# A stick-breaking attention's diagonal masks moved from Pool to VectorE, and a new order for the last expert

## The reference, cut to what matters

```python
z = einsum('bqhd,bkhd->bhqk', q, k) * SB_SCALE
visible = k_pos[None, :] < q_pos[:, None]              # strictly causal
log_skip = where(visible, log_sigmoid(-z), 0.0)
between = cumsum(log_skip, axis=3, reverse=True) - log_skip
weight = where(visible, exp(log_sigmoid(z) + between), 0.0)
out = einsum('bhqk,bkhd->bqhd', weight, v)
...
hh = silu(x @ w_gate[e]) * (x @ w_up[e]) * comb[e]      # per expert e
y = y + hh @ w_down[e]
```

## Time and profile before

| | |
|---|---|
| median of 3 runs | 870.22 us (869.53 to 870.33) |
| the profiled execution | 869.36 us |
| its span, first to last instruction | 867.6 us |
| PE busy | 820.0 us, 95% |
| DVE, ACT, POOL busy | 319.5, 233.7, 183.5 us |
| mean granted PE clock | 0.995 |
| DMA | 155.78 MB |

### The profile page before, as it was taken

The page is one execution under the profiler, slowest core; times in us unless marked ns, Lnnn a source line. Parts: engine busy times, 40 slices in busy tenths (PEclk is TensorE's granted clock), DMA queues, the critical chain, the costliest instruction groups (busy, mean ns, idle before and its releaser), DMA issues.

```text
span 867.6 us, 11942 instructions
## 1 busy us (share of the span) xinstructions
PE 820.0 (95%) x4635; PEld 504.8 (58%) x4635; DVE 319.5 (37%) x917; ACT 233.7 (27%) x483; POOL 183.5 (21%) x225
## 2 busy tenths in 40 slices
PE   6989999999899999899999999999799999999885
PEld 4465444688665765576676677455555555555452
DVE  5222555999643542122232336435621111111100
ACT  3021232112333333234333350212222222222211
POOL 3223440000332322200000001100124334343222
PEclk9999999999999999999999999999999999999998
DMA  8624020412200200210304059844789999999994
GB/s 285 170 98 129 3 99 0 151 57 94 98 1 0 98 1 0 78 28 1 146 1 97 1 189 412 321 159 149 280 308 393 397 400 398 397 395 398 401 405 146
DMA packets 59544, 155.78 MB, mean 180 GB/s; under 512 B 15384, under 2 KB 22008, under 8 KB 52320
## 3 DMA queue, kind: packets, MB, share of 16 engines
q1 hardware_dynamic: 50912, 141.74, 43.6%
q0 software_dynamic: 8576, 13.28, 5.7%
HBM read 147.10 MB, written 15.99 MB: 188 GB/s over the span
## 4 chain that ended last, share of the span: by engine, by line
PE 79%; DMA 5%; POOL 3%; DVE 3%; SPq 3%; ACT 3%; issue 2%; POOLq 0%; DVEq 0%; ACTq 0%
PE quad L866 18%; PE pair L1201 9%; PE quad L1336 6%; PE quad L1456 5%; PE pair L1456 5%; PE pair L1064 5%; PE quad L936 3%; DMA arena<-in_w_up 3%; PE pair L1469 3%; PE quad L1469 3%; PE pair L856 2%; PE quad L1158 2%; SPq L732 2%; POOL arena L1940 2%; PE pair L983 2%
## 5 line engine op out<-in xcount | busy, mean ns | idle before, releaser
L866 PE MATMUL quad<-ring_w,xnT 128*128 128x512 f32 (+1 forms) x192 | 79.3, 553 | 0.0
L1064 PE MATMUL pair<-xnT,ring_w 128*128 128x272 f32 x256 | 70.6, 411 | 0.9 <-POOLq L1946 0.9
L1201 PE MATMUL pair<-xnT,ring_w 128*128 128x272 f32 x256 | 65.8, 403 | 0.0
L2004 POOL DMA_INDIRECT out_y_prompt<-ring_w,idx x32 | 50.8, 1586 | 65.2 <-ACT ring_w L1817 63.3
L866 PE MATMUL quad<-xnT,ring_w 128*128 128x280 f32 (+1 forms) x256 | 60.6, 396 | 0.0
L1064 PEld LDWEIGHTS pair<-xnT,ring_w 128*128 128x128 f32 x256 | 46.7, 194 | 16.9 <-issue 7.9
L2247 DVE CUSTOM_DVE_ANT_0 arena<-quad,arena 128x528 f32<-128x528 f32 (+4 forms) x34 | 17.7, 520 | 103.9 <-PE quad L1256 60.9
L1201 PEld LDWEIGHTS pair<-xnT,ring_w 128*128 128x128 f32 x256 | 46.5, 189 | 15.3 <-issue 6.9
L866 PEld LDWEIGHTS quad<-xnT,ring_w 128*128 128x128 f32 x256 | 48.2, 190 | 10.8 <-issue 0.4
L1999 POOL DMA_INDIRECT ring_w<-xn_d,idx x32 | 33.2, 1038 | 95.8 <-PE quad L1447 45.9
L866 PEld LDWEIGHTS quad<-ring_w,xnT 128*128 128x128 f32 x192 | 34.3, 189 | 31.7 <-issue 26.1
(11 more groups left out here) (285 smaller groups left out, 1239.9 us busy)
## 6 DMA issues: line engine op xcount, KB each, us to landing
arena<-in_w_gate SPq DMA_DIRECT2D x21, 1024.0 KB
arena<-in_w_up SPq DMA_DIRECT2D x21, 1024.0 KB
arena<-in_w_down SPq DMA_DIRECT2D x40, 512.0 KB
ring_w<-in_w_in SPq DMA_DIRECT2D x8, 2048.0 KB, 8.5
ring_w<-in_w_down SPq DMA_DIRECT2D x20, 512.0 KB, 21.7
xnT<-in_w_gate SPq DMA_DIRECT2D x4, 1024.0 KB
xnT<-in_w_up SPq DMA_DIRECT2D x4, 1024.0 KB
ring_w<-in_w_in SPq DMA_DIRECT2D x3, 1024.0 KB, 7.3
```

The costliest lines, as they stand in the source:

```text
L866: last = nc.tensor.matmul(o, l, r, start=i == 0, stop=i == len(mms) - 1)
L1064: last = nc.tensor.matmul(bank[6 + job % 2][:, 0:hi - lo], chunk8(6 + cb // 4)[:, k, c0:c0 + P], xT[:, k, lo:hi], start=k == 0, stop=k == ...
L1201: last = nc.tensor.matmul(bank[6 + job % 2][:, 0:hi - lo], w[:, k, c0:c0 + P], rhs[:, k, lo:hi], start=k == 0, stop=k == kt - 1)
L2004: pool.indirect_dma_start(yp_half, bass.IndirectOffsetOnAxis(ap=rows, axis=0), Yb[:, q, :], None, bounds_check=2 * SEQ - 1, oob_is_err=Fal ...
```

## The change

Three things.

1. Pool masks nothing in the stage. DVE adds -1e30 (`BIG` times a 0/-1 triangle that is already in SBUF) to the masked scores in PSUM, ahead of the clamp, once per diagonal step: one instruction for a prompt step, two for the sample step and for the tail. The clamp, exp, ln and the maximum then give 0 for these elements, and so does the exponential for the weights. PE waits for `sp_ready` and `w_ready` in every step.
2. Before the gather's wait `keep_busy(6)` becomes `keep_busy(4)`.
3. For the last expert (n = 31) PE turns its hidden values between the two halves of the down product of expert 30, and does the sample's sum for expert 29 right after that product, ahead of the down product of 31.

```diff
@@ PE, stage @@
-                    if s["diag"]:
-                        pe.wait_ge(w_masked, s["diags"])
-                    else:
-                        pe.wait_ge(w_ready, m + 1)
+                    pe.wait_ge(w_ready, m + 1)
...
-                    if s["diag"]:
-                        pe.wait_ge(sp_masked, s["diags"])
-                    else:
-                        pe.wait_ge(sp_ready, m + 1)
+                    pe.wait_ge(sp_ready, m + 1)
...
-            keep_busy(6)
+            keep_busy(4)
@@ PE, experts @@
-            def down(q, slot, done):
+            def down(q, slot, done, between=None):
                 for f in range(2):
+                    if f and between is not None:
+                        between()
...
+                def turn_hidden():
+                    pe.wait_ge(hid_ready, n + 1)
+                    hidden_to_width(n % 2, hT_ready)
+                if n == NE - 1:
+                    down_in_turn(n - 1, turn_hidden)
+                    add_sample_in_turn(n - 2)
+                    break
                 if n:
                     down_in_turn(n - 1)
-                pe.wait_ge(hid_ready, n + 1)
-                hidden_to_width(n % 2, hT_ready)
+                turn_hidden()
             down_in_turn(NE - 1)
-            for n in range(NE - 3, NE):
+            for n in range(NE - 2, NE):
                 add_sample_in_turn(n)
@@ Pool, stage: mask() and its two calls are gone @@
-                    if s["diag"]:
-                        p0, p1 = s["p0"], s["p0"] + s["nk"]
-                        pool.wait_ge(sp_ready, i + 1)
-                        mask(spt[p0:p1] if s["kind"] == "tail" else spb[p0:p1, i % SPR], s)
-                        nc.gpsimd.sem_inc(sp_masked, 1)
...
-                    if s["diag"]:
-                        p0, p1 = s["p0"], s["p0"] + s["nk"]
-                        pool.wait_ge(w_ready, m + 1)
-                        mask(wtt[p0:p1] if s["kind"] == "tail" else wtb[p0:p1, m % WR], s)
-                        nc.gpsimd.sem_inc(w_masked, 1)
@@ DVE, stage @@
+            def not_before(z, s):
+                p0, p1 = s["p0"], s["p0"] + s["nk"]
+                if s["kind"] == "prompt":
+                    q0 = 0 if s["j"] else N_META
+                    w = P - q0
+                    return [(ntri[:, q0:P].rearrange("p (o q) -> p o q", o=1).broadcast_to([P, 2, w]), z[:, :, 0:w])]
+                nq = DEC if s["kind"] == "sample" else N_TAIL
+                later = ntri[p0:p1, p0:p0 + nq].rearrange("p (o q) -> p o q", o=1).broadcast_to([p1 - p0, NPAIR, nq])
+                return [(later, z[:, u, :].rearrange("p (b q) -> p b q", b=NPAIR)) for u in range(2)]
...
                 dve.wait_ge(z_ready, i + 1)
+                if s["diag"]:
+                    for later, z_diag in not_before(z, s):
+                        ins = nc.vector.scalar_tensor_tensor(z_diag, later, BIG, z_diag, ALU.mult, ALU.add)
+                    link(ins)
```

More of the change, by code:

```diff
@@ L151, in sb_steps @@
         s["closes"] = s["last"] and s["kind"] != "tail"
-        s["diags"] = sum(t["diag"] for t in steps[:i + 1])
     for i, s in enumerate(steps):
@@ L482, in build @@
         sp_ready = sem("sp_ready")
-        sp_masked = sem("sp_masked")
         suf_init = sem("suf_init")
@@ L1473, in down, with down_in_turn @@
                 last.then_inc(done, 1)
-            def down_in_turn(n):
+            def down_in_turn(n, between=None):
                 pe.wait_ge(hidT_ready, n + 1)
@@ L1479, in down_in_turn @@
                     pe.wait_ge(y_copied, n - 1)
-                down(n % 2, n % MS, y_done)
+                down(n % 2, n % MS, y_done, between)
             def add_sample(q, first, last, done):
@@ L1904, in _ @@
             pool.wait_ge(keys_out, 16 * 6 * (NT + 1))
[L1905 to L1918, removed]
-                    p0, p1 = s["p0"], s["p0"] + s["nk"]
-                    v = v.rearrange("p u (b q) -> p (u b) q", b=NPAIR)
-                    later = stri[p0:p1, p0:p1].rearrange("p (o q) -> p o q", o=1).broadcast_to([N_TAIL, 2 * NPAIR, N_TAIL])
-                    link(nc.gpsimd.tensor_tensor(v, v, later, ALU.mult))
-            for i in range(NSTEP + 1):
-                if i < NSTEP:
-                    s = STEPS[i]
-                    if s["diag"]:
-                        p0, p1 = s["p0"], s["p0"] + s["nk"]
-                        pool.wait_ge(sp_ready, i + 1)
-                        mask(spt[p0:p1] if s["kind"] == "tail" else spb[p0:p1, i % SPR], s)
-                        nc.gpsimd.sem_inc(sp_masked, 1)
+            for i in range(NSTEP + 1):
                 m = i - 1
```

## The result

| | before | after |
|---|---|---|
| median, runs of one chip | 869.88 us (869.45 to 870.33, 4 runs) | 860.13 us (859.22 to 861.20, 4 runs) |
| ratio | | 0.9885 [0.9868, 0.9903] |
| profiled execution, its span | 869.36 us, 867.6 us | 859.87 us, 858.0 us |
| PE, DVE, POOL busy | 820.0, 319.5, 183.5 us | 818.4, 327.0, 168.8 us |

The account below looks back on a forecast made before the run. TensorE and its waits bound the kernel up to the experts, the weight stream from there on. Stage 9.2 + last expert 0.55 - filler's clock fall 1.2 = 8.55 us less than 870.22: forecast 861.6 us, range 859.2 to 864.5.

Parts of the forecast that it names:

- The bound: Whole kernel: TensorE and its waits up to the experts, then the weight stream; time gained before the experts moves the end equally.
- The stalls, 8.4: Stick-breaking stage: TensorE's 13 waits for Pool vanish, 7.5 us of idle time plus 0.9 us of lost overlap.
- The clock in the stage, 1.66: Stick-breaking stage: the low clock after the longest stall (1.79 us, before 329.39) goes with that stall, gaining 1.66 us.
- The mask, 0.52 a step and 0.85 in all: VectorE's mask ahead of the clamp: 0.48 us plus 0.04 wait per step, costing 0.85 us where ScalarE's slack is short.
- the three places: Stage steps with little ScalarE idle time before its weights (226.28, 284.70, 326.40): would pay 0.52, 0.10 and 0.24 us.
- The filler, -1.2: Before the gather: two fewer filler calls lengthen TensorE's idle to 2.6 us, the clock likely falls, costing 1.2 us (0 to 1.7).
- rival 1: At the gather: the clock holds despite the longer idle gap, giving 860.4 us; chance 0.32.
- The last expert, 0.55: Kernel's end: ScalarE's copy of y(31) no longer waits for the sample's sum of expert 29, gaining 0.55 us (0 to 0.9).
- The sum: Whole kernel: 9.2 for the stage + 0.55 for the last expert - 1.2 for the filler = 8.55 us less.
- Rival 4: Stage: the added mask paces every step, slower than before from a mask of about 3.2 us, about 880 at 3.5; chance 0.02.

Follow-up runs that it names:

- the filled stall: Kernel before, with throwaway products filling the longest stall (1.8 us, step 17's product with the values), the wait itself kept: 869.66 us, ratio 0.9989.
- four masks: Changed kernel with VectorE's mask issued four times in each diagonal step, the masked values unchanged: 873.95 us, ratio 1.0042 against the kernel before.

## Why the prediction was right, step by step

**The bound.** Right. From the gate and up product of the second expert to the last scatter it took 225.1 us before (634.25 to 859.37) and 224.6 to 225.3 in the thirteen other profiles, although it began at times between 624.1 and 635.5. What is gained or lost before the experts arrives at the end.

**The stalls, 8.4.** Right, and confirmed from two sides: the wait for Pool vanished, and turning Pool's order alone brought 8.05, the clock's share included. Put side by side, instruction by instruction, the two profiles give 8.63 for the stalls: 7.65 us of idle time and 14 times the 0.07 of overlap. The one that I hadn't counted is at 346.07, with 0.12 us too short for a bracket.

**The clock in the stage, 1.66.** Measured 1.65 by the filled stall.

**The mask, 0.52 a step and 0.85 in all.** It took 0.43 + 0.03 = 0.46. The price in the stage is 0.64, the difference to the kernel that keeps it off ScalarE's chain. Two of the three places paid, 0.24 and 0.40 where I had about 0.5 and 0.24; at the third (282.15, before: 284.70) ScalarE's idle time went to nothing, and TensorE didn't wait. The stage adds up: 8.63 + 1.65 - 0.64 is 9.64, and 9.62 was measured where I had 9.2.

**The filler, -1.2: the step that failed.** I let the clock fall after 2.6 us of idle time and took 1.2 us off the gain. The gap was 2.46 us and the clock held, as in rival 1 (860.4, with a chance of 0.32; 860.13 was measured). So the forecast of 861.6 stood for the wrong one of the two cases, and is near because the case was worth little. The filler alone gave 1.0003, with 3.06 us of gap and no fall. The price was of the right size, if low (1.4 to 1.7 in the four profiles where a low clock reached the experts' start); the cause was not.

Idle times just before the gather and what followed, by profile: 1.65, 1.71, 2.00, 2.46 and 3.06 us passed, 1.70, 1.81 and 1.89 were followed by a fall. The length of the gap does not order these. (In five of the other six the clock had fallen in or just before the filler, which then took longer and left 0 to 0.9 us; from the gather to the second gate and up product these took the full-clock 6.54, so a fall there cost nothing. The sixth is the 4.99.)

Over the whole of the 14 profiles, after the first 20 us, 10 of the 28 idle times of TensorE of 1.75 to 3.1 us that began at full clock were followed by a fall, and 1 of the 46 of 1.5 to 1.75. So the length does count, and by this count a fall at 2.46 us was a chance of about a third and not likelier than not. In 11 of the 14 profiled executions the clock was low for a time between 604 and 632 us, in three of them twice, at different places for the same program, and 11 of the falls there had no idle time over 0.82 us just before them. Against that, the 1.8 us stall at 330 was followed by a fall in all three profiles that have it.

The Trainium skill ("TensorE: Matmul & The Clock Gate", section "What's actually happening") says that the point of a transition depends on when the work arrives against a monitor that runs freely; the two profiles of the changed kernel agree with that, since at 612.5 the same idle times were followed by a fall in one and not in the other. By the rule on gaps of the same page of the Trainium skill (section "Why this matters for your kernels"), weighed in the prediction, 2.46 us was safe: so it was in this trace, but 2.16 us at 808 in the same trace was not, nor were 1.70 to 1.89 us in the others.

**The last expert, 0.55.** The mechanism gave 0.54 from the start of the product of 30 on. What I left out is when that product starts. I had put the last expert after the arrival of the last weights, but the product of 30 waits for its own w_down, which lands last but one. In the change's first profile that made it start 0.24 us later after the gate and up product than before, so 0.30 net; in its second profile 0.03 later, and 0.51 net. Between the five profiles with the old last expert (10.06 to 10.38 us from gate and up to scatter) and the eight with the split (9.53 to 9.84) the means differ by 0.54. The upper bound of 0.9 wasn't there to be had: the 0.39 us of idle time before the product of 31 ends at 855.40, and the weights of 31 had landed at 855.23, so at most 0.1 us of it could go.

**The sum.** 9.62 + 0.30 is 9.92 where I had 8.55, or 9.75 without the filler's term; the other stretches took 0.32 more, so the spans differ by 9.6. That this is so near 9.75 is in part luck: 0.4 more in the stage, 0.25 less in the last expert and 0.32 lost elsewhere nearly cancel.

**Rival 4's turning point was wrong.** I put it at a mask of 3.2 us by dividing the mean slack of 2.8 evenly. With four masks, 1.8 us a step, the stage had already lost 9.2 of its 9.6 us, and the median was slower than before (1.0042). The narrow steps have 1.2 us of slack and pay first, and a wait that a mask creates can bring the clock down as Pool's did.

## What to carry to other kernels

When one engine's result waits behind that engine's other duty, first ask for the order: masking before adding would have brought 8 of the stage's 9.6 us without a new operation. When work is moved onto a chain, sum the slack step by step and not by its mean; a side job (here the mask of the scores) can often run while the next engine works. A clock fall behind a gap near 2 us is a chance (here 10 in 28) and not a term: take it out of the central forecast unless several profiles show it at that place. And before you reorder the end of a kernel, look up when its last weights land.

## What the runs showed of the hardware

- VectorE's scalar_tensor_tensor with input and output in PSUM took 429 ns for 128x256 and 396 for 128x224; a tensor_tensor from PSUM to SBUF of 128x256 took 424.
- The place of a low clock changes between executions of one program, and with it TensorE's time by 1.4 to 1.7 us where nothing hides it. The mean granted clock of the kernel before was 0.987 to 0.995 over 48 executions, 0.991 at the median; with the stall filled it was 0.992 to 0.998 over 10.
- Of 28 idle times of TensorE of 1.75 to 3.1 us, 10 were followed by a low clock; of 46 of 1.5 to 1.75 us, one. Eleven more falls came among short products and throwaway ones with no idle time over 0.82 us just before.
- Around 4.99 us of idle time the clock was low for over 10 us on end; it had fallen 0.7 us before the idle time began.
- Expert 31's w_down landed 2.50 us after expert 30's in all 14 profiles, and the product of expert 30 started 0.09 us after the landing that it waited for.
- The time before the stage, the same code in all, was 221.3 to 224.6 us in the profiles, while the stage repeated within 0.05 us wherever its code was the same.
